# Six of ten norm openings: the row scaling moves from VectorE into TensorE's turn, by a diagonal matrix

## The reference

```python
def rms_norm(x, g):
    xf = x.astype(jnp.float32)
    y = xf * lax.rsqrt(jnp.mean(xf * xf, axis=-1, keepdims=True) + RMS_EPS)
    return (y * g.astype(jnp.float32)).astype(x.dtype)
...
# first block: hn = rms_norm(h, ln_mix[i]); z = hn @ a_w_in
#              h = h + swiglu(rms_norm(h, ln_ffn[i]), w1, w3, w2)
#              gate = sigmoid(rms_norm(h, ln_ple[i]) @ ple_gate[i])
# second block: h = rmsnorm(x, norm_mix_g[l]) * (1.0 + sc1) + sh1; z = h @ w_in[l]
#               h = rmsnorm(x, norm_mlp_g[l]) * (1.0 + sc2) + sh2; relu(h @ w_up)**2 @ w_down
```

## Time and profile before

| | |
|---|---|
| time, median of 3 runs | 2026.6 us (2026.26 to 2028.07) |
| time of the profiled execution | 2026.65 us, span 2024.9 us |
| busy: PE / DVE / ACT / POOL | 1942.2 / 1558.7 / 1198.0 / 28.2 us |
| PE's share of the span | 96% |
| mean granted TensorE clock | 0.982 of 2.4 GHz |

### The profile page before, as it was taken

The page is one execution under the profiler, slowest core; times in us unless marked ns, Lnnn a source line. Parts: engine busy times, 40 slices in busy tenths (PEclk is TensorE's granted clock), DMA queues, the critical chain, the costliest instruction groups (busy, mean ns, idle before and its releaser), DMA issues.

```text
span 2024.9 us, 27801 instructions
## 1 busy us (share of the span) xinstructions
PE 1942.2 (96%) x10958; PEld 1668.3 (82%) x10958; DVE 1558.7 (77%) x2130; ACT 1198.0 (59%) x1649; POOL 28.2 (1%) x32
## 2 busy tenths in 40 slices
PE   7999999999999999999999999799999989999998
PEld 7889998777878787878787877698789978878997
DVE  5768886758898989898989898667388985736555
ACT  4444445436777777777777777566354446634443
POOL 0000000000000000000000000000000000000000
PEclk9999999999999999999999999999899999989999
DMA  7348886537899989898989999343158974314551
GB/s 304 142 157 336 330 329 231 177 115 283 341 347 340 350 338 352 337 351 335 354 339 349 341 347 359 134 146 125 60 218 329 358 275 144 126 54 157 187 190 47
DMA packets 71694, 513.08 MB, mean 253 GB/s; under 512 B 8194, under 2 KB 8578, under 8 KB 10114
## 3 DMA queue, kind: packets, MB, share of 16 engines
q1 hardware_dynamic: 69536, 504.40, 65.9%
q10 hardware_dynamic: 2020, 6.82, 1.0%
HBM read 510.14 MB, written 1.05 MB: 252 GB/s over the span
## 4 chain that ended last, share of the span: by engine, by line
PE 82%; DVE 11%; ACT 5%; issue 1%; POOL 1%; DMA 0%; ACTq 0%; POOLq 0%; SPq 0%; DVEq 0%
PE ps L532 25%; PE ps L534 24%; PE ps L533 24%; DVE w_lo L1323 6%; ACT w_hi L2183 2%; PE ps L751 2%; PE ps L952 2%; PE ps L541 1%; PE ps L703 1%; PE ps L717 1%; PE ps L970 1%; POOL stat L2670 1%; DVE resid L1925 1%; ACT xT L2193 0%; DVE x_lo L1912 0%
## 5 line engine op out<-in xcount | busy, mean ns | idle before, releaser
L2183 ACT ACTIVATE w_hi<-ring 128x1024 fp32r<-128x1024 f32 x862 | 911.9, 1061 | 658.0 <-PE ps L534 651.3
L1323 DVE TENSOR_TENSOR w_lo<-ring,w_hi 128x1024 fp32r<-128x1024 f32 x862 | 1042.1, 1222 | 328.0 <-ACT w_hi L2183 303.7
L532 PE MATMUL ps<-w_hi,x_hi 128*128 128x512 f32 (+1 forms) x1056 | 410.0, 391 | 11.4 <-DVE w_lo L1323 3.5
L534 PE MATMUL ps<-w_hi,x_lo 128*128 128x512 f32 (+1 forms) x1056 | 401.0, 382 | 0.0
L533 PE MATMUL ps<-w_lo,x_hi 128*128 128x512 f32 (+1 forms) x1056 | 400.2, 381 | 0.0
L532 PE MATMUL ps<-x_hi,w_hi 128*128 128x256 f32 x1248 | 360.0, 288 | 4.8 <-DVE x_lo L1438 3.6
L533 PE MATMUL ps<-x_lo,w_hi 128*128 128x256 f32 x1248 | 355.4, 285 | 0.0
L534 PE MATMUL ps<-x_hi,w_lo 128*128 128x256 f32 x1248 | 355.3, 285 | 0.0
L532 PE MATMUL ps<-w_hi,h_hi 128*128 128x512 f32 x732 | 291.5, 398 | 7.8 <-DVE h_lo L1919 7.8
L533 PE MATMUL ps<-w_lo,h_hi 128*128 128x512 f32 x732 | 285.3, 390 | 0.0
L534 PE MATMUL ps<-w_hi,h_lo 128*128 128x512 f32 x732 | 285.0, 389 | 0.0
(11 more groups left out here) (269 smaller groups left out, 1421.6 us busy)
## 6 DMA issues: line engine op xcount, KB each, us to landing
ring<-in_stream SPq DMA_DIRECT2D x479, 1024.0 KB, 4.9
con<-in_consts ACTq DMA_DIRECT2D x1, 2048.0 KB, 23.0
arena<-in_ln_rows ACTq DMA_DIRECT2D x3, 512.0 KB, 4.4
resid<-in_x SPq DMA_DIRECT2D x1, 1024.0 KB, 5.9
arena<-in_c ACTq DMA_DIRECT2D x2, 512.0 KB, 3.6
arena<-in_fin_row ACTq DMA_DIRECT2D x2, 512.0 KB, 3.9
out<-rows SPq DMA_DIRECT2D x2, 512.0 KB, 2.6
arena<-in_w_s ACTq DMA_DIRECT2D x1, 512.0 KB, 8.0
```

Of the source, the lines that this page charges most:

```text
L532: pe.matmul(out_, lhs[0], rhs[0], start=start, stop=False)
L534: return pe.matmul(out_, lhs[1], rhs[0], start=False, stop=stop)
L1323: dve.tensor_tensor(lo, ring[:, q % RING, a:a + HALF], hi.bitcast(F32), ALU.subtract)\
L2183: act.activation(half_buffer(m)[0], ring[:, q % RING, a:a + HALF], ACT.Copy).then_inc(hi_ready, 1)
```

## The change

For norms 0, 1, 6, 7, 8 and 9 the scaled copy is no longer made. VectorE writes a 128x128 diagonal matrix with the roots of the row block, `diag[:, t, :]` = identity x root, and TensorE multiplies the raw rows by it, so that turning and scaling are one fp32 matmul for each tile. Norm 4 keeps its copy, norms 2, 3 and 5 have none. TensorE waits two times instead of three in each of the six norms.

```diff
+DIAGONAL = (0, 1, 6, 7, 8, 9)
-SCALED_AT = {k: 3 * i for i, k in enumerate(k for k in range(10) if k not in RAW)}
+SCALED_AT = {0: 0, 1: 2, 4: 4, 6: 7, 7: 9, 8: 11, 9: 13}
...
+        diag = sb("diag", [P, QB, P])
...
                 def turn(t, f):
                     at = ps[:, 4 + f // 2, (f % 2) * S + t * P:(f % 2) * S + (t + 1) * P]
                     c = slice(f * P, (f + 1) * P)
-                    return pe.transpose(at, (resid if k == 6 or k in RAW else rows)[:, t, c], ident)
+                    if k in DIAGONAL:
+                        return pe.matmul(at, (rows if k == 6 else resid)[:, t, c], diag[:, t, :], start=True, stop=True)
+                    return pe.transpose(at, (resid if k in RAW else rows)[:, t, c], ident)
 
                 def scaled(n):
                     if k in RAW:
                         pe.wait_ge(resid_ready, 4 * (k - 1) + 1 + n)
-                    else:
+                    elif n < 3 or k not in DIAGONAL:
                         pe.wait_ge(rows_scaled, SCALED_AT[k] + n)
...
                     r = stat[:, 2 * t + 1:2 * t + 2] if k == 6 else stat[:, t:t + 1]
-                    src, dst = (rows, resid) if k == 6 else (resid, rows)
...
-                    for c in [slice(0, D)] if t == 0 else [slice(0, BANK), slice(BANK, D)]:
-                        dve.tensor_scalar(dst[:, t, c], src[:, t, c], r, None, ALU.mult).then_inc(rows_scaled, 1)
+                    dve.tensor_scalar(diag[:, t, :], ident, r, None, ALU.mult).then_inc(rows_scaled, 1)
```

## The result

| | before | changed |
|---|---|---|
| first measurement, median | 2026.88 us (2023.28 to 2028.73, 6 runs) | 2032.84 us (2030.59 to 2037.0, 6 runs), ratio 1.0029, 95% interval 1.0016 to 1.0042 |
| again (`after_again`) | 2027.16 us (33 runs) | 2030.27 us (11 runs), ratio 1.0014, 1.0003 to 1.0024 |
| a third time (`after_third`) | 2028.69 us (35 runs) | 2030.65 us (12 runs), ratio 1.0014, 1.0004 to 1.0024 |
| profiled execution, span | 2024.9 us | 2028.8 us |

The change makes the kernel slower by 0.1 to 0.3%. All three intervals lie above 1. The forecast was no change, 2024.2 to 2029.6 us; the median lies above that range.

The account below looks back on a forecast made before the run. TensorE was taken as the bound, 82% of the chain that ended last. The places summed 0.95 + 0.2 + 1.1 - 1.7 + 1.1 - 1.7 = -0.05 us: forecast 2026.6 us, range 2024.2 to 2029.6.

Parts of the forecast that it names:

- norm 0: Start of the program: sixteen matmuls, clock back about 13.0, second half slot up to 17.8; +0.95 us, bounds +0.5 and +1.7.
- norms 7 and 9: MLP of both late layers: wait behind the burst filled by matmuls, no clock fall expected; -1.7 us each, -3.4 for both.
- norm 1: FFN: the burst of matmuls ends at 135.08 against a first product at 134.60; +0.2 us, bounds 0 and +0.5.
- norm 6: First late layer: burst of twelve matmuls mostly at 1.2 GHz, first product 1.7 late; +1.1 us, bounds +0.35 and +1.7.
- norm 8: Second late layer, no warming matmuls: doubling the burst at 1.2 GHz lands on the path; +1.1 us, same bounds as norm 6.
- Prices: Diagonal matmul 0.223 us at full clock, 0.427 at half, two records; diagonal write 0.28; second burst starts 0.20 earlier.
- Rival (d): All bursts: a matmul on raw rows costs 0.44 us at full clock, not 0.223; +12.8 us, 2039.4; chance 0.03.
- rival (a): Norms 7 and 9: the clock falls as before; +2.4 us, 2029.0; chance 0.27.
- (b): Norms 7 and 9: the burst itself runs at 1.2 GHz, +1.0 us each; sum +5.35, 2032.0; chance 0.06.
- (c): Norms 0, 6 and 8: matmuls keep the clock up, transposes do not, so it returns earlier; -2.0 us, 2024.6; chance 0.13.
- the last line of my forecast: Stretches the change doesn't touch: a shift of a microsecond may move clock falls there, 1 or 2 us either way.

Follow-up runs that it names:

- the early order: Changed kernel, all eight tiles of row block 0 turned behind the first wait: 2026.5 us, ratio 0.9993; with diagonals in norms 6 to 9 alone 2025.66 us.
- eye: Kernel before, scaled copy kept but turned by an fp32 matmul with the identity in norms 0, 1, 6, 7, 8, 9; 2032.7 us, ratio 1.0027.
- raw6789: Kernel before, but norms 6 to 9 wait for the diagonal and transpose raw rows, leaving out the roots' scaling; 2025.83 us, ratio 0.9994.
- warm_before2: Second run of the kernel before with products without use added in TensorE's waits of norms 6 and 8, no diagonals; ratio 1.0007 to before.
- d79: Diagonals in norms 7 and 9 alone, the other norms keeping the scaled copy of the kernel before; ratio 0.9987.
- warm_d6789: Kernel before with diagonals in norms 6 to 9 and products without use added in TensorE's waits of norms 6 and 8; ratio 0.9988.

## Why the prediction was wrong

- **The sum's terms.** Mean opening with diagonal against mean with scaled copy, in the traces without the added warming products and without the early order (norm 0, where sixteen tiles stand ahead of the first product in all of them, also takes those; in norms 7 and 9 every trace serves except those of `eye` and `raw6789`):

| | predicted | measured | from |
|---|---|---|---|
| norm 0 | +0.95 | +1.9 | 17.25 (11 traces) to 19.1 (6) |
| norm 1 | +0.2 | +0.3 | 10.28 to 10.60 |
| norm 6 | +1.1 | +1.0 | 17.7 (5) to 18.7 (5) |
| norm 8 | +1.1 | +1.1 | 13.8 (5) to 14.9 (5) |
| norms 7 and 9 | -3.4 | -2.6 | 13.9 and 13.6 (7 each) to 12.4 and 12.5 (9 each) |
| sum | -0.05 | +1.7 | |

- **Prices: right.** 0.22 us for each matmul, two records, 0.28 for a diagonal, 0.20 earlier for the burst. Rival (d) is out: the factor is 3.65/1.76 = 2.07. The Trainium skill ("TensorE: Matmul & The Clock Gate", the glossary ahead of Part 1, under xbus) says four, and the traces do not agree.
- **Norms 1, 6 and 8: right.** For 6 and 8 the early order and the warmed kernel show the mechanism, a long burst at half clock. Its length varies more than I took: 4.57 to 5.49 us in the ten bursts of five traces, since in three of the norm 6 bursts the clock was still at 2.4 GHz when the burst began and fell within it.
- **Norm 0: mis-sized, the step that failed first (+0.95 taken, +1.9 measured).** The prediction took the return of the clock from one trace, at 13.0, as a fixed moment. By the starts of TensorE's records, 0.21 us apart at half clock and 0.11 to 0.12 at full, it returned at 12.5 in that trace, but anywhere from 12.5 to 15.8 in the eleven with the scaled copy and from 12.7 to 15.1 in the six with the diagonal. The scaled copy hardly feels that (openings of 16.9 to 17.5 us); the doubled burst does (18.4 to 19.9). The chain behind the burst was short as well. In `after_again` the clock was back at 12.7 and the first product came at 14.71, as forecast, yet the second half slot started at 18.37 and not at 17.8: four `x_hi` of 0.4 us stood behind the last pairs of tiles, where I had 0.8 us, so the eighth ended at 16.12 (forecast 15.7) and the last `x_lo` at 17.08 (16.55). ScalarE's first weight split, which I had left out, ended level with that, at about 17.05. Against the mean with the scaled copy the second half slot is 1.1 to 2.7 us late in the six traces; the upper bound of 1.7 was too low.
- **Norms 7 and 9: mechanism right, size off.** I took -1.7 each, from the trace of before, in which the clock fell behind both bursts. In seven traces with the scaled copy it fell in 10 of 14 openings. Without a fall the diagonal gains only 13.0 - 12.4 = 0.6 us. It fell in none of 18 openings with a diagonal, nor in the two of `eye`, so rival (a) is out. That the filled wait is what holds the clock is an inference from these counts: `raw6789` shows that it can hold without. That the trace of before had a fall behind both bursts was chance, and the step that failed here is that I priced it as if every execution had it.
- **Rivals (b) and (c).** (b), the burst of 7 and 9 at 1.2 GHz, occurred in no trace: in the first trace norm 7's burst took 2.94 us, at full clock. The slower outcome came by norm 0 instead. (c) asked for an earlier return of the clock in norms 6 and 8, with bursts of 3.6 us; the shortest of the ten took 4.57.
- **The range.** It had the bounds of the openings and none for the rest of the program. Single executions of the changed kernel lie between 2024.6 and 2037.0 us. The clock falls at other moments in stretches that the change does not touch, as the last line of my forecast said and its range did not. The first measurement's +5.9 us stands 3 us above the two later ones; with these, the change costs some 1 to 5 us, of which 1.7 are accounted for by openings. In the three traces 1.4, 3.1 and 3.9 us lie between the openings, against one trace of before. Whether that is more than spread stays open.

## What to carry to other kernels

Folding a per-row scale into the turn trades a write of 1024 columns on VectorE for a second record for each tile on TensorE: it pays where TensorE waits behind the turn (norms 7 and 9, 2.5 us faster by themselves) and costs where the turn is already level with the rest (norm 0, and norms 6 and 8 at half clock). Turn what is ready in the wait ahead, so that the burst behind the last scale is short; where there is no wait ahead, as in norm 1, that order costs (0.5 us). A gain read from one trace that contains a fall of the clock is worth the fall's frequency, not the fall.

## What the runs showed of the hardware

- Keeping TensorE busy in a wait ahead of transposes gained nothing in three of six openings (17.8, 13.7 and 13.7 us, as before) and in the other three moved the fall of the clock behind the wait, where it cost 1.0 to 1.2 us. One kernel so treated measured 1.0013 (1.0004 to 1.0022), again 1.0007 (0.9992 to 1.0022).
- At the start of the program the clock came back at different moments in kernels that are alike up to there: 12.5 to 15.8 us from the start of the span in eleven traces whose first burst is sixteen transposes.
- Executions of one kernel spread by up to 14 us (`warm_before2`, 2023.4 to 2037.7). In the runs beside `after_again` 30 of 33 of before lie within 2025.5 to 2028.5 us and the changed kernel's 11 from 2024.6 to 2034.7; in those beside `after_third` before itself spreads from 2024.6 to 2035.0.
- No run here is clearly better than `d79` and `warm_d6789`, both 0.12% faster than before (intervals to 0.9977 and 0.9979).
